# The weight ring skips the place that holds the memory's tokens, and the queries' weights are loaded ahead of the tokens

## What is computed

```python
h = rms_norm(x, norm_mix_w[i])
mem_n = rms_norm(mem, mem_norm_w[i])
proj = h @ nsa_w_in[j]
mix = nsa_mixer(proj[..., :NSA_COLS], ...)      # 8 heads, three branches each
qm = proj[..., NSA_COLS:]
mo = memory_attention(qm.reshape(B, S, MEM_HEADS, HEAD_DIM), mem_n, mem_w_kv[i])
x = x + jnp.concatenate([mix, mo], axis=-1) @ w_out[i]
x = x + conv_glu(rms_norm(x, norm_ffn_w[i]), ffn_w_up[i], ffn_conv_w[i], ffn_conv_b[i], ffn_w_down[i])

def memory_attention(qm, mem_n, w_kv):
    kv = (mem_n @ w_kv).reshape(B, -1, 2, MEM_HEADS, HEAD_DIM)
    k, v = kv[:, :, 0], kv[:, :, 1]
    s = jnp.einsum('bshd,bmhd->bhsm', qm, k) * HEAD_DIM ** -0.5
    p = jax.nn.softmax(s, axis=-1)
    return jnp.einsum('bhsm,bmhd->bshd', p, v)
```

## Time and profile before

| | us |
|---|---|
| three timed runs | 2762.47, 2765.56, 2774.45 |
| their median | 2765.56 |
| profiled execution | 2757.81 |
| its span in the trace | 2756.0 |
| TensorE busy in it | 2502.6 |
| VectorE, ScalarE busy | 894.3, 522.6 |

### The profile page before, as it was taken

One profiled execution on the slowest core, in us unless ns is written; L12 is line 12 of the kernel. 1 busy time (PEld: TensorE's weight loads), 2 busy tenths in 40 slices (PEclk: granted clock), 3 DMA queues, 4 the chain that ended last, 5 costly groups with the idle time before them and its releaser, 6 DMA issues.

```text
span 2756.0 us, 28361 instructions
## 1 busy us (share of the span) xinstructions
PE 2502.6 (91%) x11512; PEld 1632.4 (59%) x11512; DVE 894.3 (32%) x2139; ACT 522.6 (19%) x1149; POOL 51.9 (2%) x79
## 2 busy tenths in 40 slices
PE   8989699999997999998878999999898879999997
PEld 6878558856863886577644444444677544444443
DVE  4366428431152654335331111111433331111112
ACT  2132311001251100124311111111314221111111
POOL 0000000000100000002000000000020000000000
PEclk9989899999999999999989999999899989999999
DMA  8310056675604677443138999999542239999995
GB/s 308 107 61 1 1 190 253 244 274 150 204 1 165 249 257 291 153 154 121 35 119 349 398 410 419 393 415 395 198 157 79 77 136 419 404 417 409 418 411 246
DMA packets 148880, 653.81 MB, mean 237 GB/s; under 512 B 14538, under 2 KB 20938, under 8 KB 124032
## 3 DMA queue, kind: packets, MB, share of 16 engines
q1 hardware_dynamic: 145600, 642.98, 59.5%
q0 software_dynamic: 3136, 8.86, 1.3%
HBM read 648.67 MB, written 3.15 MB: 237 GB/s over the span
## 4 chain that ended last, share of the span: by engine, by line
PE 83%; DVE 9%; issue 3%; ACT 2%; DMA 1%; SPq 1%; DVEq 0%; ACTq 0%
PE ps L106 81%; DVE AR L125 3%; PE ps L109 2%; ACT AR L115 1%; SPq L101 1%; DVE AR L120 1%; DMA wring<-in_nsa_w_in 1%; DMA wring<-in_w_out 0%; DVE SM L137 0%; DVE AR L133 0%; DVE AR L129 0%; DVE X L125 0%; DVE SM L145 0%; DVE AR L121 0%; ACT L115 0%
## 5 line engine op out<-in xcount | busy, mean ns | idle before, releaser
L106 PE MATMUL ps<-wring,AR 128*64 128x512 f32 (+3 forms) x3776 | 930.6, 585 | 73.4 <-issue 52.8
L106 PE MATMUL ps<-HT,wring 128*128 128x256 f32 x3200 | 726.7, 389 | 2.7 <-DMA wring<-in_nsa_w_in 1.5
L106 PEld LDWEIGHTS ps<-wring,AR 128*64 128x64 f32 (+2 forms) x3776 | 372.4, 145 | 598.9 <-issue 593.7
L106 PEld LDWEIGHTS ps<-HT,wring 128*128 128x128 f32 x3200 | 623.0, 196 | 98.6 <-issue 6.4
L115 ACT ACTIVATE AR<-ps 128x512 f32<-128x512 f32 (+6 forms) x274 | 138.4, 505 | 1048.1 <-PE ps L106 587.7
L106 PE MATMUL ps<-AR 128*128 128x128 f32 (+6 forms) x1288 | 284.2, 370 | 26.0 <-DVE AR L125 16.4
L125 DVE TENSOR_TENSOR AR<-ps,AR 128x512 f32<-128x512 f32 (+2 forms) x120 | 67.1, 559 | 662.9 <-PE ps L106 658.2
L106 PEld LDWEIGHTS ps<-AR 128*128 128x128 f32 (+4 forms) x1288 | 178.7, 192 | 120.6 <-issue 81.3
L106 PE MATMUL ps<-AR,XN 128*128 128x128 f32 x1024 | 124.4, 281 | 4.5 <-DVE AR L125 4.5
L129 DVE SCALAR_TENSOR_TENSOR wring<-wring,CC 128x512 f32<-128x512 f32 x168 | 126.3, 752 | 6.0
L109 PE MATMUL ps<-CS,AR 128*128 128x128 f32 (+2 forms) x474 | 80.0, 291 | 51.4 <-DVE AR L120 26.3
(11 more groups left out here) (149 smaller groups left out, 1352.7 us busy)
## 6 DMA issues: line engine op xcount, KB each, us to landing
wring<-in_w_gate SPq DMA_DIRECT2D x64, 2048.0 KB, 13.8
wring<-in_w_up SPq DMA_DIRECT2D x64, 2048.0 KB, 9.9
wring<-in_w_down SPq DMA_DIRECT2D x64, 2048.0 KB, 12.3
wring<-in_w_ada SPq DMA_DIRECT2D x24, 2048.0 KB, 10.9
wring<-in_ffn_w_up SPq DMA_DIRECT2D x20, 2048.0 KB, 10.9
wring<-in_w_in SPq DMA_DIRECT2D x18, 2048.0 KB, 7.6
wring<-in_w_out SPq DMA_DIRECT2D x10, 2048.0 KB, 7.7
wring<-in_ffn_w_down SPq DMA_DIRECT2D x10, 2048.0 KB, 12.6
```

Source lines behind the costliest of these rows:

```text
L106: return Ins(self.eng and self.eng.matmul(out, lhs, rhs, start=start, stop=stop), None)
```

## The change

`Ring` keeps a list of places in place of a counter, and `defer` sends the next place to the end of the list without giving it to anyone. In `sync`, the queries' weights are named ahead of the tokens, and the ring skips one place ahead of chunk 2 of `out1`.

```diff
     def restart(self):
-        self.n, self.held = 0, [None] * len(self.places)
+        self.order, self.held = list(range(len(self.places))), [None] * len(self.places)
+
+    def defer(self):
+
+        self.order.append(self.order.pop(0))
 
     def take(self, name):
-        i = self.n % len(self.places)
-        self.n += 1
+        i = self.order[0]
+        self.defer()
         self.where[name], self.before[name], self.held[i] = i, self.held[i], name
         return self.places[i]
...
-        def project(name, src, chunks):
-            for c in range(chunks):
+        def project(name, src, chunks, first=0):
+            for c in range(first, chunks):
                 weights((name, c), src[c * 512:c * 512 + 512], 4, 1024)
...
+        weights(("qm", 1), win[:, 2584:3096], 8, 512)
         memory(1)
-        weights(("qm", 1), win[:, 2584:3096], 8, 512)
         memory_kv(1)
-        project("out1", t["w_out"][1], 3)
+        project("out1", t["w_out"][1], 2)
+        W.defer()
+        project("out1", t["w_out"][1], 3, 2)
         ffn(1)
```

## The result

| | before | changed |
|---|---|---|
| first timing, median | 2765.31 (4 runs) | 2738.78 (4 runs) |
| first timing, lowest to highest | 2762.47 to 2774.45 | 2734.69 to 2744.71 |
| profiled execution | 2757.81, span 2756.0 | 2738.46, span 2736.6 |
| all timings of this study, mean | 2758.3 (64 runs) | 2742.3 (21 runs) |

The first timing gives a ratio of 0.99 with a 95% interval of 0.9871 to 0.9929. The two profiled executions differ by 19.4.

What follows compares the result with a forecast made beforehand. TensorE's idle at the output projection, its w_out chunks held until place 2 was free, was taken as the bound. 12.87 + 2.1 + 1.4 = 16.4 us off the median of 2765.56 gave 2749.2, range 2740 to 2760.

Steps and rivals of the forecast that it cites:

- What bounds, and why: Output projection, layer 1: TensorE idles 12.87 us for w_out chunks 1 and 2, held until place 2 is free.
- Part 1, idle 12.87: Ahead of the output projection's last group: skipping a place loads both chunks early and removes 12.87 us of idle.
- Part 1, low clock 2.1: Output projection's last group: the low clock after the idle goes too, saving 2.1 us.
- The copy of the last output, and the feed-forward's chunks 1 and 2: VectorE's copy of the memory's last output is 3 us early; feed-forward chunk 1 lands 11.8 early, chunk 2 is covered.
- Part 2, 1.4: At the second query projection: queries' weights ahead of the tokens remove TensorE's 1.53 us wait, gaining 1.4 us.
- The wait of 0.8 at the turn: After the queries, TensorE waits 0.8 us for VectorE's copy of the hidden units, delayed by the later tokens.
- The sum: Whole kernel: 12.87 + 2.1 + 1.4 = 16.4 us saved.
- The base: Whole kernel: 16.4 us taken off the median of 2765.56, not the profiled 2757.81, giving 2749.2.
- The clock's case: Output projection: the 2.1 us of low clock stay and a 1.7 us slow stretch is added: 2753.0; chance 0.12.
- The late tokens: Memory of layer 1: tokens keep their 26.8 us landing, TensorE waits 9.5 us, 3.4 gained: 2762.2; chance 0.07.
- nothing moves: Output projection: the place passed over isn't the blocking one, or another holds the chunks: 2765.6 or 2764.2; chance 0.05.
- chunk 1 is late: Feed-forward's second chunk: its load needs 36.9 us, TensorE waits 17.3 and loses 2.1 of clock: 2768.6; chance 0.04.

Runs made afterwards that it cites:

- ffn_late: Changed kernel with two more places skipped ahead of the feed-forward, so its chunk 0 waits for the output projection's end: 2752.40 (12 runs).
- before_cut: Kernel before, shortened to 2 of the 16 pairs of experts in each layer: 1901.13 (5 runs).
- after_cut: Changed kernel, shortened to 2 of the 16 pairs of experts in each layer: 1883.04 (5 runs).
- before_turned: Kernel before with its five ring places laid out one further on in memory, waits and order untouched: 2759.02 (12 runs), ratio 1.0.
- tokens_late_cut: Changed kernel, shortened to 2 of 16 expert pairs per layer, with the tokens one more load behind, after the keys' weights: 1887.46.
- part2_alone: Kernel before with only the queries' weights put ahead of the tokens, no place skipped: 2754.93 (12 runs), ratio 0.9994.
- e_after: Changed kernel, unaltered, timed again with more rounds beside the kernel before: 2746.85 (11 runs), ratio 0.9958.

## Why the prediction was right or wrong

**What bounds, and why: right.** The stall was one place that held two loads back. With it free, TensorE's idle is gone and no other took its place there.

**Part 1, idle 12.87: right.** Between the memory's last output and the last group, the four traces of kernels with neither part of the change have 12.9 to 13.1, nine with both chunks early have none.

**Part 1, low clock 2.1: right in kind, 0.4 short.** From the last group's start to the last turn ahead of the feed-forward, the four have 33.5 to 34.7 (mean 34.0), every trace of the changed kernel 31.6: 1.9 to 3.1, on average 2.5. Part 1 as a whole is 15.6 with that, above the 15.0 that the prediction called the most.

**The copy of the last output, and the feed-forward's chunks 1 and 2: right.** The copy ends at 849.6 for a first use at 852.4. Chunk 1 landed 8.0 after its issue (7.8 was the row), chunk 2 after 25.1 (at most 32.7 was said, 35.6 needed). ffn_late shows that the margin was real: with it taken away, TensorE waits.

**Part 2, 1.4: the direction right, the term too small.** The tokens' landing was forecast at 732.4, 5.1 us after TensorE's start on the hidden units (727.27), and came at 734.2, 5.1 after 729.14. By the clock's face that is past the 734 that was named as a sign of being wrong; it is the whole trace that runs 1.9 later at this point. The wait of 0.8 at the turn is 1.02, 0.73, 1.00 and 0.87 in four traces; in the profiled execution of the changed kernel it is absent, since the hidden units ran at a low clock (5.12 instead of 3.70) and hid it. From the hidden units' end to the last memory output, the mean is 117.6 in the four and 114.9 in the changed kernel's five, 2.7 instead of 1.4. The rest came behind the turn. Stretches of the granted clock there, before_cut and after_cut:

```profile
744.00:748.00 4.00, 3.18 (x12) 2.79 (x11) 1.46 (x9) 3.66 (x8) 0.00 (x0) 0.62 0.52 205
748.00:752.00 4.00, 4.00 (x12) 3.26 (x11) 0.97 (x6) 2.71 (x12) 0.00 (x0) 0.53 0.00 0
```

```profile
740.00:744.00 4.00, 2.65 (x16) 2.12 (x17) 1.48 (x9) 3.55 (x8) 0.00 (x0) 1.00 1.03 407
744.00:748.00 4.00, 4.00 (x21) 3.54 (x20) 0.96 (x6) 3.71 (x13) 0.00 (x0) 1.00 0.26 103
```

Behind its string of short waits the old order of the two loads (the skip alone has it too) has a low clock in five of six traces, the new order in one of seven (ffn_late, 0.71 and 0.87, with 116.5 instead of 114.9). The sixth of the old order is before_turned: its hidden units ran slow and there was no wait for the queries' weights:

```profile
732.80 4.81 PE L106 MATMUL ps<-wring,AR 128*32 128x128 f32 x128
737.64 7.17 PE L106 MATMUL ps<-HT,wring 128*128 128x256 f32 x32
```

It has the full clock behind and takes 115.0, as the changed kernel does. So the 2.7 is a mean: 2.6 to 4.7 where the wait for the weights is there, nothing where it isn't. The prediction had row 748.29 with its 7.50 in hand, where like rows take 7.07, and didn't ask why. Why the one string of waits mostly drops the clock and the other mostly doesn't stays open.

**The sum: 16.4 against 18.3 by these terms** (13.1 + 2.5 + 2.7). The whole stage differs by 19.1 between the means of four and five traces (246.3 and 227.2). By time it is 16.0 in the full kernels (2758.3 less 2742.3) and 21 in the shortened. The standard error of the 16.0 would be 1.5 if all runs were alike, but they aren't: the changed kernel's mean is 2746.5 in the second timing and 2736.7 in the last, on another chip, and in the three timings that have both kernels in full the means differ by 27.6, 10.6 and 21.8, on average 20.0. So the gain lies between some 15 and 21, and the forecast of it was right or a few us low.

**The base: this is the step that failed.** The prediction saw that the profiled execution lay 7.75 below the median of the three runs, took the median as base, and got 2749.2. The 64 runs of before have a mean of 2758.3: the three shown were 7 high, and the profiled 2757.81, which was set aside, was at the middle. The same sum from it gives 2741.4, as the text also says, and the 21 runs of the changed kernel have 2742.3. So of the 10.4 us between the forecast and the first timing's 2738.8, 7.3 are the base, 1.9 are terms that were too small (0.2, 0.4 and 1.3), and 1.2 are left for the scatter. By medians (2758.2 and 2743.0 over all timings) the first timing's 26.5 is 15.2 of effect, 7.1 of a high base, and 4.2 of four runs of the changed kernel that came out low. That the first timing's runs of before were high by chance is likely and not shown: their mean is 9.1 above that of the other 60, with a standard error of 2.9, and whether the chip that they ran on has to do with it stays open.

**The range: too narrow for its own numbers.** "The runs shown spread over 12" was given as its reason, but single kernels here run over 20 us (2748 to 2770). It should have reached 8 us lower, to the base at the profiled execution.

**The rivals.** The clock's case (2753.0) didn't come as such, but its mechanism, a low clock without a stall of the stage's own, is what the scatter of the runs goes with. The Trainium skill ("TensorE: Matmul & The Clock Gate", Part 1: The HAM clock gate) was cited for a slow stretch after idle that varies between runs. The page speaks of a kernel's start; the runs agree further on. Behind the stall the slow stretch was there in all of the four traces, but its cost went from 1.9 to 3.1, and in the experts it comes in one run and not in the next. The late tokens did not come, and tokens_late_cut shows what 5 us more would have cost, some 4. That nothing moves, and that chunk 1 is late, are excluded by the traces.

**Gain carried to the end: right as far as can be told.** The experts' two stretches together had 1072.5 and 1073.5 in traces of the old order, and 1065.9, 1079.4 and 1063.2 in those of the changed kernel. With 16 between the latter, five traces show no term there that belongs to the change, nor do they rule out one of a few us.

## What to carry to other kernels

In a ring that is filled in order, look for the tenant with the longest stay: everything named behind its successor waits with it, and skipping one place, at the price of a little less prefetch once, can free two loads. Before skipping, list which load inherits which wait, and compare its landing with the time to its first use; here 19.6 us against 8.0 made it free, and with 4.3 it cost 10.

Choose the base of a forecast as carefully as the difference. If the profiled execution and the median of a few runs differ by half the expected effect, the range has to hold both.

## What the runs showed of the hardware

A wait in a loop that is bound by loads costs more than itself when the clock falls behind it. An ordinary pair of experts took 29.8 to 31.0 us; with a wait of 2.2 to 3.4 and a full clock 31.2 to 32.4; with a wait of 2.7 to 3.6 and the low clock for its next matmuls (8.5 to 9.7 instead of 7.1) 33.4 to 35.3. At the same wait it is the slow matmuls and nothing more that the pair is longer by. With these rows the pair took 32.0 in part2_alone and 33.65 in e_after:

```profile
2371.68 7.09 PE L106 MATMUL ps<-wring,AR 128*64 128x512 f32 x32 [2.98 <-issue]
```

```profile
1687.66 8.72 PE L106 MATMUL ps<-wring,AR 128*64 128x512 f32 x32 [2.99 <-issue]
```

The eight traces have one to six such pairs each, some 3.5 us longer than an ordinary one. The changed kernel's three, with 1, 2 and 6, had spans of 2732.4, 2736.6 and 2744.6. That such pairs make most of the scatter of 20 us over all runs fits this and the clock's correlation, but isn't shown for the runs without a trace. Which pairs are hit changes from trace to trace, with one exception: the pair that ends at 1508 to 1526 is long in seven of the eight.
